# Group norm of a state-space mixer: the root and the reciprocal move from a 128x16 tile into whole PSUM banks, and the halves of the output projection are exchanged

## The chip, the core and the metric

The kernel runs on one core of a Trainium2 chip. The metric is the device time in microseconds (us), here the median of the runs shown. Five engines work side by side and wait for one another through semaphores: TensorE (PE, matrix products, with its weight loads shown as PEld), VectorE (DVE), ScalarE (ACT), GpSimd (POOL), and SyncE (SP), which here only issues transfers. Each engine takes its instructions in the order written.

## The reference, cut to what matters

The program is two transformer-like blocks on 512 tokens of width 1024; the change lies in the second one, in the norm over groups that closes the state-space branch and in the product that follows:

```python
y = y.reshape(b, L, D_INNER) * jax.nn.silu(z)                  # D_INNER = 2048
yg = y.reshape(b, L, N_GROUPS, D_INNER // N_GROUPS)            # 4 groups of 512
yg = yg * lax.rsqrt(jnp.mean(yg * yg, axis=-1, keepdims=True) + NORM_EPS)
y = yg.reshape(b, L, D_INNER) * ssm_norm_w
y_ssm = y @ w_ssm_out                                          # 2048 x 1024
merged = sigmoid(g_conv) * y_conv + sigmoid(g_ssm) * y_ssm
return merged @ w_out
```

## The kernel before, in words

**Layout.** Everything is held transposed: the 128 partitions are features, the 512 columns of a tile are the tokens. A chunk is 128 features. `y_ssm` has 16 chunks, four to each group, so a group's sum of squares goes over four chunks and over the partitions.

**Weights and products.** All weights come as one stream of panels of 128x2048 fp32 (1 MB), in the order written in `weight_stream`. SP loads panel p into slot p % 2 (L418) as soon as panel p - 2 is used up by POOL. ACT rounds it to `w_hi` (`round_weights`, L1259), and POOL then writes the rest, `w_lo = w_raw - w_hi`, in four pieces (L454) and signals after the last. Operands are split in the same way: ACT writes `b_hi` or `a_hi`, DVE writes `b_lo` or `a_lo`. A tile of 128x512 outputs over eight chunks is then 24 matmuls: 16 with `w_hi` (L504 and L505) and 8 with `w_lo` (L511), 5.44 us together. It needs `w_hi` at its first matmul and `w_lo` at its 17th. Two tiles use one panel. Where an operand is just becoming ready, `tile_pair` runs both tiles of a panel together, chunk by chunk: 16 matmuls with `hi` (L542), 16 with `w_lo` (L551), 16 with `lo` (L558). Results go round four PSUM banks `gemm_bank`, and a bank has to be emptied before it is used again. The other four banks, `aux`, serve all else.

**Order around the change.** It is written out by hand, engine by engine. PE: eight tiles of the convolution's projection (panels `P_CONV` + 0 to 3), four gate tiles (`P_GATE2` + 0, 1), then the state-space output projection: the pair and six tiles over `b_hi`/`b_lo` (`P_SSM` + 0 to 3, results `T_SSM` + 0 to 7) and as much over `a_hi`/`a_lo` (`P_SSM` + 4 to 7), then the last projection. Before, the first of these halves takes `y_ssm` chunks 8 to 15, the second chunks 0 to 7; DVE adds the two results (L2376), so their order changes nothing but rounding.

**The group norm before.** ACT squares the four chunks of group m (L1653), DVE adds them (L2343), and PE sums over the partitions with the squares as the stationary operand and one column of ones moving, four matmuls of 128x1 per group (`group_sum`, L1081). All four groups' sums land in 16 columns of `aux[0]`, tokens on the partitions. Once all are there, ACT takes the root of 128x16 (L1670) and DVE the reciprocal (L2349). PE then spreads each column over a bank again, as a product of the broadcast column with the identity: eight matmuls for groups 2 and 3 after the first two gate tiles (L1102), eight for groups 0 and 1 after the last gate tile (L1110). DVE multiplies `y_ssm` by weight and spread factor (`y_operand`, L2356), ACT rounds (L1682 into `b_hi`, L1685 into `a_hi`), DVE takes the low part (L2360).

**What stands in ACT's queue here.** After each of the first two panels of its gates, ACT does two sigmoids from the banks (L1677), `round_weights`, then four chunks of `b_hi` (L1682). After these come all eight `a_hi` (L1685), and only behind them the copies of `T_SSM` + 0 and 1 (L1690) and the rounding of panel `P_SSM` + 2. `after(p, t)` is `round_weights` for panel p + 2.

Of the kernel before, what the change touches and what calls it, by code (L numbers as in the profile page):

```python
# [9 lines left out]
ACT = mybir.ActivationFunctionType  # L10
# [3 lines left out]
P = 128  # L14
S = 512
D = 1024
KC = D // P
# [3 lines left out]
QT = S // P  # L21
# [4 lines left out]
GROUPS = 4  # L26
# [69 lines left out]
def build(nc, x_in, w_in, cols_in, poolw_in, ada_in, c_in, out):  # L96

    A_USE_SSM = 4 * KC
    A_USE_FFN = A_USE_SSM + KC
    B_USE_CONV = KC + MLP_GROUPS * KC  # L100
    B_USE_SSM = B_USE_CONV + KC
# [3 lines left out]
    with ExitStack() as ctx:  # L105
        def sb(name, shape, dt=F32):
            return ctx.enter_context(nc.sbuf_tensor(name, shape, dt))

        def sem(name):
            return ctx.enter_context(nc.semaphore(name))  # L110
# [83 lines left out]
        shift_out = new_part[:, 0:2]  # L194
        rinv2 = sb("rinv2", [P, QT])
        one_gain2 = sb("one_gain2", [P, 2])
        group_inv = sb("group_inv", [P, GROUPS * QT])
        group_root = sb("group_root", [P, GROUPS * QT])
        sq = sb("sq", [P, 2, S])
        dist_at = nc.sbuf_base  # L200
        row_b = sb("row_b", [P, 2, S])
# [24 lines left out]
        eps = sb("eps", [P, 2])  # L226
# [132 lines left out]
        ln_silu = sem("ln_silu")  # L359
        groot_ready = sem("groot_ready")  # L360
        ginv_ready = sem("ginv_ready")
        gspread_done = sem("gspread_done")
        yop_raw = sem("yop_raw")
        gc_ready = sem("gc_ready")
        gs_ready = sem("gs_ready")
# [131 lines left out]
        def _(pe):  # L497
# [578 lines left out]
            def group_sum(m):  # L1076
                pe.wait_ge(group_step, 3 * m + 3)
                if m == 0:
                    pe.wait_ge(root_ready, 6)
                for j in range(QT):  # L1080
                    mm = pe.matmul(aux[0][:, 4 * m + j:4 * m + j + 1], y_sq[0][:, j * P:(j + 1) * P], ones[:, 0:1],  # L1081
                                   start=(m == 0 and j == 0), stop=(m == 3 and j == QT - 1), skip_group_check=True)
                mm.then_inc(sq_read, 1)

            for m in range(4):
                full(P_CONV + m, T_CONV + 2 * m, b_hi, b_lo,
# [4 lines left out]
            for m in range(2):  # L1091
                if m == 0:
                    tile(0, P_GATE2, T_GATE2, 0, 0, wide(0), a_hi, a_lo, first=True)
                    group_sum(3)
                    tile(0, P_GATE2, T_GATE2 + 1, 0, 0, wide(1), a_hi, a_lo)
                else:
                    full(P_GATE2 + m, T_GATE2 + 2 * m, a_hi, a_lo)
                if m == 0:
                    pe.wait_ge(ginv_ready, 1)
                    for q in (2, 3):  # L1100
                        for j in range(QT):
                            mm = pe.matmul(aux[q][:, j * P:(j + 1) * P],  # L1102
                                           group_inv[:, 4 * q + j:4 * q + j + 1].to_broadcast([P, P]), ident[:, :],
                                           start=True, stop=True)
                        mm.then_inc(gspread_done, 1)
            pe.wait_ge(centered, 8)
            pe.wait_ge(ln_raw, 8)
            for q in (0, 1):
                for j in range(QT):
                    mm = pe.matmul(aux[q][:, j * P:(j + 1) * P],  # L1110
                                   group_inv[:, 4 * q + j:4 * q + j + 1].to_broadcast([P, P]), ident[:, :],
                                   start=True, stop=True)
                mm.then_inc(gspread_done, 1)

            for m in range(4):
                full(P_SSM + m, T_SSM + 2 * m, b_hi, b_lo,
# [136 lines left out]
        def _(act):  # L1253
# [9 lines left out]
            def load_table(func):  # L1263

                nonlocal tables
                act.activation(table_out[:, tables:tables + 1], eps[:, 0:1], func)
                tables += 1
# [391 lines left out]
            for j in range(4):  # L1659
                t = T_GATE + j  # L1660
                act.wait_ge(bank_free[t % 4], free_value(t))
                act.activation(g_ssm[:, j, :], g_ssm[:, j, :], ACT.Sigmoid).then_inc(gs_ready, 1)
            for m in range(4):
                if m:
                    after(P_CONV + m, T_CONV + 2 * m)
                if m < 3:
                    group_squares(m + 1)
            load_table(ACT.Sqrt)
            act.wait_ge(sq_read, GROUPS)
            act.activation(group_root[:, :], aux[0][:, 0:GROUPS * QT], ACT.Sqrt, bias=eps[:, 0:1],  # L1670
                           scale=1.0 / (4 * P)).then_inc(groot_ready, 1)

            for m in range(2):
                for j in range(2):
# [91 lines left out]
        def _(dve):  # L1766
# [566 lines left out]
                                  ALU.subtract).then_inc(b_lo_ready, 1)  # L2333
            gated_outputs(GROUPS - 1)

            for k in range(KC):
                t = T_CONV + k
                if k % 2 == 0:
                    for n in range(1, 4):
                        dve.wait_ge(sq_ready, 4 * KC + 2 * k + n)  # L2340
                        if n > 1:
                            dve.wait_ge(group_step, 3 * (k // 2) + n - 1)
                        dve.tensor_tensor(y_sq[0], y_sq[0], y_sq[n], ALU.add).then_inc(group_step, 1)  # L2343
                dve.wait_ge(gc_ready, k + 1)
                dve.wait_ge(tile_done, t + 1)
                dve.tensor_tensor(g_conv[:, k, :], g_conv[:, k, :], gemm_bank[t % 4][:, :], ALU.mult) \
                    .then_inc(bank_free[t % 4], 1)
            dve.wait_ge(groot_ready, 1)
            dve.reciprocal(group_inv[:, :], group_root[:, :]).then_inc(ginv_ready, 1)  # L2349

            def y_operand(first, value, hi, hi_sem, hi_base, lo, lo_sem, spreads):

                dve.wait_ge(gspread_done, spreads)
                for k in range(KC):
                    f = first + k
                    dve.scalar_tensor_tensor(value[:, k, :], y_ssm[:, f, :], col("ssm_norm_w", f),  # L2356
                                             aux[f // 4][:, :], ALU.mult, ALU.mult).then_inc(yop_raw, 1)
                for k in range(KC):
                    dve.wait_ge(hi_sem, hi_base + k + 1)
                    dve.tensor_tensor(lo[:, k, :], value[:, k, :], hi[:, k, :].bitcast(F32),  # L2360
                                      ALU.subtract).then_inc(lo_sem, 1)

            dve.wait_ge(ln_silu, KC)
            dve.wait_ge(tile_done, T_GATE2)
            y_operand(8, b_raw, b_hi, b_hi_ready, B_USE_SSM, b_lo, b_lo_ready, 2)
            dve.wait_ge(tile_done, T_SSM)
            dve.wait_ge(b_lo_ready, B_USE_SSM + 1 + KC)
            y_operand(0, a_raw, a_hi, a_hi_ready, A_USE_SSM, a_lo, a_lo_ready, 4)

            for k in range(KC + 1):  # L2370
                if k < KC:
# [145 lines left out]
def panels(w, kc, mc):  # L2517

    n = w.shape[1] // (mc * P)
    return w.reshape(kc, P, n, mc * P).transpose(2, 1, 0, 3).reshape(n, P, kc * mc * P)  # L2520
# [8 lines left out]
def weight_stream(v):  # L2529

    def pick(w, chunks):
        return np.concatenate([w[:, c * P:(c + 1) * P] for c in chunks], axis=1)

    w_in, up, down = v["w_in"], v["w_up"], v["w_down"]
    stream = [panels(pick(w_in, [4 + i, 8 + i, 12 + i, i] + [16 + 4 * i + j for j in range(4)]), KC, 2)
              for i in range(PAIRS)]
    stream += [panels(v["w_branch_attn"], 4, 4), panels(v["w_branch_pool"], 4, 4), panels(v["w_out"], KC, 2)]
    for g in range(MLP_GROUPS):
        stream += [panels(up[:, g * D:(g + 1) * D], KC, 2), panels(down[g * D:(g + 1) * D, :], KC, 2)]
    w = v["w_in_2"]  # L2540
    z0, x0 = 16, 32
    dt0 = (x0 + 24) * P
    dt = np.zeros((D, 2 * P), np.float32)
    dt[:, 0:SSM_HEADS] = w[:, dt0:dt0 + SSM_HEADS]
    stream.append(panels(dt, KC, 2))
    gates = w[:, dt0 + SSM_HEADS:]
    for g in range(GROUPS):
        stream.append(panels(pick(w, [2 * g, 8 + 2 * g, 2 * g + 1, 8 + 2 * g + 1]
                                  + [x0 + 4 * g + j for j in range(4)] + [x0 + 16 + g, x0 + 20 + g]), KC, 2))
        stream.append(panels(pick(gates, [2 * g, 2 * g + 1]), KC, 2))  # L2550
        stream.append(panels(pick(w, [z0 + 4 * g + j for j in range(4)]), KC, 2))
    stream += [panels(pick(gates, range(8, 12)), KC, 2), panels(v["w_conv_out_2"], KC, 2),
               panels(pick(gates, range(12, 16)), KC, 2),
               panels(v["w_ssm_out_2"][D:], KC, 2), panels(v["w_ssm_out_2"][:D], KC, 2), panels(v["w_out_2"], KC, 2)]
    ffn, ffn_down = v["w_ffn_in_2"], v["w_ffn_down_2"]
    for g in range(FFN_GROUPS):
        chunks = range(FC * g, FC * g + FC)
        stream.append(panels(pick(ffn, [c + half for c in chunks for half in (0, FFN_GROUPS * FC)]), KC, 2))
        rows = np.zeros((16 * P, D), np.float32)
        rows[:FC * P] = ffn_down[FC * P * g:FC * P * (g + 1)]  # L2560
        stream.append(panels(rows, 16, 1))
    return np.ascontiguousarray(np.concatenate(stream, axis=0))
# [51 lines left out]
```

## Time and profile before

| | |
|---|---|
| time, median of 3 runs | 1696.14 us (1695.92 to 1697.41) |
| profiled execution, span | 1694.9 us; its own time outside the span isn't given, the median lies 1.24 us above the span |
| PE busy | 1684.5 us, 99% of the span |
| DVE, ACT, POOL busy | 52%, 42%, 47% |
| granted TensorE clock, mean | 0.997 |
| stretch of the change | about 1130 to 1245 us from the span's start |

The span is the time from the first to the last instruction of one execution, recorded by the profiler. "Busy" counts work only, not waits. Durations of neighbouring matmuls overlap, since they are pipelined, so what a matmul costs is read from the distance between starts, not from its own duration. Bracketed text at the end of a timeline row is the idle time before the instruction, and what ended it.

### The profile page before, as it was taken

Reading aid. Unit: us, or ns where it says so; the run is one execution under the profiler, and the core shown is the slowest. Engines: PE = TensorE matmul, PEld = TensorE weight load, DVE = VectorE, ACT = ScalarE, POOL = GpSimd, SP = SyncE. Lnnn points to the kernel's source line nnn. Section 1 sums busy time; section 2 is a strip of 40 time slices with the busy share of each in tenths; the row PEclk is TensorE's granted clock in tenths of the full one; section 3 lists DMA queues with packets and bytes.
Section 4 is the critical chain, followed back from the end, with each engine's and each line's share of the span. In section 5 each row is a group of like instructions: output and inputs, shape, how many; then the busy total and the mean of one; then the engine's idle time right before and its main releaser. Section 6 shows DMA issues by size and latency. Waiting matters only on the chain.

```text
span 1694.9 us, 21874 instructions
## 1 busy us (share of the span) xinstructions
PE 1684.5 (99%) x7963; PEld 1374.6 (81%) x7963; DVE 874.7 (52%) x1365; ACT 706.1 (42%) x977; POOL 793.1 (47%) x605
## 2 busy tenths in 40 slices
PE   9999999999999999999999999999999999999998
PEld 7777778788888888888878888788888888888887
DVE  6234374563616167797897878863355511101113
ACT  5333364431313134456464554784424422222232
POOL 2434354444545455543434344444545544654453
PEclk9999999999999999999999999999999999999999
DMA  5222222274636342233222332222222222332232
GB/s 187 99 75 74 74 104 82 81 261 157 229 117 225 122 151 100 93 106 125 100 100 101 117 104 99 99 75 99 76 99 100 76 98 99 129 127 91 99 124 100
DMA packets 32540, 193.84 MB, mean 114 GB/s; under 512 B 3648, under 2 KB 5696, under 8 KB 13792
## 3 DMA queue, kind: packets, MB, share of 16 engines
q1 hardware_dynamic: 25376, 158.89, 26.5%
q10 hardware_dynamic: 7104, 34.15, 5.8%
q8 instruction: 38, 0.62, 0.1%
q14 instruction: 22, 0.18, 0.0%
HBM read 190.86 MB, written 2.16 MB: 114 GB/s over the span
## 4 chain that ended last, share of the span: by engine, by line
PE 98%; DMA 0%; DVE 0%; ACT 0%; SPq 0%; issue 0%; DVEq 0%
PE gemm_bank L511 25%; PE gemm_bank L504 25%; PE gemm_bank L505 25%; PE gemm_bank L542 4%; PE gemm_bank L558 4%; PE gemm_bank L551 3%; PE gemm_bank L546 1%; PE gemm_bank L789 1%; PE aux_bank L975 1%; PE aux_bank L655 1%; PE aux_bank L980 1%; PE aux_bank L960 1%; PE aux_bank L681 1%; PE aux_bank L672 1%; DMA w_raw<-weights_dram 0%; PE aux_bank L953 0%
## 5 line engine op out<-in xcount | busy, mean ns | idle before, releaser
L454 POOL TENSOR_TENSOR w_lo<-w_raw,w_hi 128x512 fp32r<-128x512 f32 x580 | 771.5, 1362 | 881.6 <-ACT w_hi L1259 870.4
L504 PE MATMUL gemm_bank<-a_hi,w_hi 128*128 128x512 f32 x1008 | 402.6, 399 | 0.0
L505 PE MATMUL gemm_bank<-a_lo,w_hi 128*128 128x512 f32 x1008 | 393.2, 390 | 0.0
L1259 ACT ACTIVATE w_hi<-w_raw 128x2048 fp32r<-128x2048 f32 x145 | 276.5, 1907 | 187.1 <-PE gemm_bank L511 122.7
L504 PE MATMUL gemm_bank<-b_hi,w_hi 128*128 128x512 f32 x688 | 267.8, 389 | 0.0
L505 PE MATMUL gemm_bank<-b_lo,w_hi 128*128 128x512 f32 x688 | 267.7, 389 | 0.0
L511 PE MATMUL gemm_bank<-a_hi,w_lo 128*128 128x512 f32 x1024 | 258.7, 395 | 0.0
L511 PEld LDWEIGHTS gemm_bank<-a_hi,w_lo 128*128 128x128 f32 x1024 | 190.2, 188 | 45.0 <-issue 6.2
L504 PEld LDWEIGHTS gemm_bank<-a_hi,w_hi 128*128 128x128 f32 x1008 | 189.3, 188 | 43.9 <-issue 5.6
L505 PEld LDWEIGHTS gemm_bank<-a_lo,w_hi 128*128 128x128 f32 x1008 | 189.4, 188 | 39.4 <-issue 1.9
L2161 DVE SCALAR_TENSOR_TENSOR aux_bank<-scratch,gcol,aux_bank 128x511 f32<-128x511 f32 (+15 forms) x240 | 165.8, 734 | 14.2 <-ACT aux_bank L1485 11.9
L511 PE MATMUL gemm_bank<-b_hi,w_lo 128*128 128x512 f32 x688 | 170.6, 389 | 0.0
L511 PEld LDWEIGHTS gemm_bank<-b_hi,w_lo 128*128 128x128 f32 x688 | 129.1, 188 | 26.8
L505 PEld LDWEIGHTS gemm_bank<-b_lo,w_hi 128*128 128x128 f32 x688 | 129.2, 188 | 26.8
L504 PEld LDWEIGHTS gemm_bank<-b_hi,w_hi 128*128 128x128 f32 x688 | 129.1, 188 | 26.7
L2461 DVE TENSOR_TENSOR arena<-arena,gemm_bank 128x512 f32<-128x512 f32 x21 | 14.4, 688 | 174.6 <-PE gemm_bank L511 173.1
L2394 DVE SCALAR_TENSOR_TENSOR h<-gemm_bank,mod,h 128x512 f32<-128x512 f32 x23 | 17.3, 751 | 108.6 <-PE gemm_bank L511 104.9
L504 PE MATMUL gemm_bank<-f_hi,w_hi 128*128 128x512 f32 x165 | 64.2, 389 | 0.0
L505 PE MATMUL gemm_bank<-f_lo,w_hi 128*128 128x512 f32 x165 | 64.2, 389 | 0.0
L1735 ACT ACTIVATE f_hi<-arena 128x512 f32 (+1 forms) x22 | 13.9, 632 | 115.9 <-DVE arena L2461 115.0
L2202 DVE SCALAR_TENSOR_TENSOR sq<-gemm_bank,gcol,sq 128x511 f32<-128x511 f32 (+2 forms) x72 | 53.8, 748 | 13.2 <-ACT sq L1505 11.5
L1393 ACT ACTIVATE b_hi<-gemm_bank 128x512 fp32r<-128x512 f32 x31 | 18.6, 599 | 100.5 <-DVE gemm_bank L2006 100.5
(414 smaller groups left out, 2133.4 us busy)
## 6 DMA issues: line engine op xcount, KB each, us to landing
w_raw<-weights_dram SPq DMA_DIRECT2D x146, 1024.0 KB, 4.7
arena<-ada_dram ACTq DMA_DIRECT2D x32, 768.0 KB, 4.7
acc<-cum_rows ACTq DMA_DIRECT2D x8, 512.0 KB, 3.7
h<-x_t_dram SPq DMA_DIRECT2D x8, 256.0 KB, 5.9
row_b<-cum_rows ACTq DMA_DIRECT2D x4, 512.0 KB, 4.8
scratch<-cum_rows ACTq DMA_DIRECT2D x4, 512.0 KB, 4.2
out_t_dram<-a_raw SPq DMA_DIRECT2D x7, 256.0 KB, 2.2
w_raw<-weights_dram SPq DMA_DIRECT2D x4, 256.0 KB, 5.2
```

The costliest lines, as they stand in the source:

```text
L454: ins = pool.tensor_tensor(wlo[s][:, w], raw[s][:, w], whi[s][:, w].bitcast(F32), ALU.subtract)
L504: pe.matmul(gemm_bank[bank][:, :], whi[slot][:, w], hi[:, k, :], start=(n == 0), stop=False)
L505: pe.matmul(gemm_bank[bank][:, :], whi[slot][:, w], lo[:, k, :], start=False, stop=False)
L511: mm = pe.matmul(gemm_bank[bank][:, :], wlo[slot][:, blk * P:blk * P + P], hi[:, k, :], start=False, stop=(n == last))
L542: pe.matmul(gemm_bank[t % 4][:, :], whi[panel % 2][:, w], hi[:, k, :], start=(n == 0), stop=False)
L551: pe.matmul(gemm_bank[t % 4][:, :], wlo[panel % 2][:, blk * P:blk * P + P], hi[:, k, :], start=False, stop=False)
L558: mm = pe.matmul(gemm_bank[t % 4][:, :], whi[panel % 2][:, blk * P:blk * P + P], lo[:, k, :], start=False, stop=(n == last))
L1259: act.activation(whi[panel % 2][:, :], raw[panel % 2][:, :], ACT.Copy).then_inc(w_hi_ready, 1)
L1393: act.activation(b_hi[:, j, :], bank, ACT.Square).then_inc(b_hi_ready, 1)
L2161: dve.scalar_tensor_tensor(aux[q][:, d:S], u_buf[:, q, 0:S - d], gc(G_CONV_W + CONV_TAPS * q + CONV_TAPS - 1 - d), aux[q][:, d:S], ALU.mul ...
L2202: ins = dve.scalar_tensor_tensor(acc[:, d:S], bank[:, 0:S - d], gc(G_SSM_W + SSM_TAPS * n + SSM_TAPS - 1 - d), acc[:, d:S], ALU.mult, ALU.add)
L2394: dve.scalar_tensor_tensor(hk, gemm_bank[t % 4][:, :], g_, hk, ALU.mult, ALU.add).then_inc(h_ready, 1)
```

## The change

- `group_sum(m)` becomes one product per group: 128x128 ones as the stationary operand, the 128x512 sum of squares moving, into the whole bank `aux[m]`. Each partition of the bank then holds the sum for each token, so nothing has to be spread. For m = 1 PE waits also for `ln_raw` (the bank's readers of before).
- ACT takes the root in the bank, in place, 128x512, once per group; `group_root(m)` stands behind `group_squares(m + 1)`, and the load of the table for the root stands ahead of the loop.
- DVE takes the reciprocal in the bank, in place, 128x512, once per group: groups 0 and 1 within the loop over the convolution's tiles (after k = 3 and k = 5), groups 2 and 3 between the two calls of `y_operand`.
- The sixteen matmuls that spread the factors are gone, with their semaphore.
- The first half of the output projection (operand b) takes chunks 0 to 7, the second (operand a) chunks 8 to 15, and the weight stream exchanges the two halves of `w_ssm_out_2`.

```diff
@@ PE
-                for j in range(QT):
-                    mm = pe.matmul(aux[0][:, 4 * m + j:4 * m + j + 1], y_sq[0][:, j * P:(j + 1) * P], ones[:, 0:1],
-                                   start=(m == 0 and j == 0), stop=(m == 3 and j == QT - 1), skip_group_check=True)
-                mm.then_inc(sq_read, 1)
+                if m == 1:
+                    pe.wait_ge(ln_raw, KC)
+                pe.matmul(aux[m][:, :], ones[:, :], y_sq[0], start=True, stop=True).then_inc(sq_read, 1)
...
-                if m == 0:
-                    pe.wait_ge(ginv_ready, 1)
-                    for q in (2, 3):
-                        for j in range(QT):
-                            mm = pe.matmul(aux[q][:, j * P:(j + 1) * P],
-                                           group_inv[:, 4 * q + j:4 * q + j + 1].to_broadcast([P, P]), ident[:, :],
-                                           start=True, stop=True)
-                        mm.then_inc(gspread_done, 1)
-            pe.wait_ge(centered, 8)
-            pe.wait_ge(ln_raw, 8)
-            for q in (0, 1):
...                                      (the same eight matmuls for groups 0 and 1)
@@ ACT
+            def group_root(m):
+                act.wait_ge(sq_read, m + 1)
+                act.activation(aux[m][:, :], aux[m][:, :], ACT.Sqrt, bias=eps[:, 0:1], scale=1.0 / (4 * P)) \
+                    .then_inc(groot_ready, 1)
+
+            load_table(ACT.Sqrt)
             for m in range(4):
                 if m:
                     after(P_CONV + m, T_CONV + 2 * m)
                 if m < 3:
                     group_squares(m + 1)
-            load_table(ACT.Sqrt)
-            act.wait_ge(sq_read, GROUPS)
-            act.activation(group_root[:, :], aux[0][:, 0:GROUPS * QT], ACT.Sqrt, bias=eps[:, 0:1],
-                           scale=1.0 / (4 * P)).then_inc(groot_ready, 1)
+                group_root(m)
@@ DVE
+            def group_inverse(m):
+                dve.wait_ge(groot_ready, m + 1)
+                dve.reciprocal(aux[m][:, :], aux[m][:, :]).then_inc(ginv_ready, 1)
...
-            dve.wait_ge(groot_ready, 1)
-            dve.reciprocal(group_inv[:, :], group_root[:, :]).then_inc(ginv_ready, 1)
+                if k in (3, 5):
+                    group_inverse(k // 2 - 1)
...
-            y_operand(8, b_raw, b_hi, b_hi_ready, B_USE_SSM, b_lo, b_lo_ready, 2)
+            y_operand(0, b_raw, b_hi, b_hi_ready, B_USE_SSM, b_lo, b_lo_ready, 2)
+            group_inverse(2), group_inverse(3)
             dve.wait_ge(tile_done, T_SSM)
             dve.wait_ge(b_lo_ready, B_USE_SSM + 1 + KC)
-            y_operand(0, a_raw, a_hi, a_hi_ready, A_USE_SSM, a_lo, a_lo_ready, 4)
+            y_operand(8, a_raw, a_hi, a_hi_ready, A_USE_SSM, a_lo, a_lo_ready, 4)
@@ weight_stream
-               panels(v["w_ssm_out_2"][D:], KC, 2), panels(v["w_ssm_out_2"][:D], KC, 2), panels(v["w_out_2"], KC, 2)]
+               panels(v["w_ssm_out_2"][:D], KC, 2), panels(v["w_ssm_out_2"][D:], KC, 2), panels(v["w_out_2"], KC, 2)]
```

## Rows read from the trace of the kernel before

**Rows 1.** The page: busy time of each engine, and the granted clock by slices.
```profile
PE 1684.5 (99%) x7963; PEld 1374.6 (81%) x7963; DVE 874.7 (52%) x1365; ACT 706.1 (42%) x977; POOL 793.1 (47%) x605
...
PEclk9999999999999999999999999999999999999999
```

**Rows 2.** Waits of PE over the whole span: total, times, longest, in us.
```profile
PE gemm_bank L789 <- ACT a_hi L1371: 1.4, 1, 1.4
...
PE aux_bank L1214 <- ACT sq L1759: 0.9, 1, 0.9
```

**Rows 3.** Timeline of PE, group sums and first spread: start, us, engine, line, operation.
```profile
1142.69 1.98 PE L511 MATMUL gemm_bank<-b_hi,w_lo 128*128 128x512 f32 x8
1148.13 1.98 PE L511 MATMUL gemm_bank<-b_hi,w_lo 128*128 128x512 f32 x8
1149.95 0.95 PE L1081 MATMUL aux_bank<-ones,sq 128*128 128x1 f32 x8
1154.49 1.98 PE L511 MATMUL gemm_bank<-b_hi,w_lo 128*128 128x512 f32 x8
...
1172.65 1.98 PE L511 MATMUL gemm_bank<-a_hi,w_lo 128*128 128x512 f32 x8
1174.47 1.95 PE L1102 MATMUL aux_bank<-ident,group_inv 128*128 128x128 f32 x16
1179.91 1.98 PE L511 MATMUL gemm_bank<-a_hi,w_lo 128*128 128x512 f32 x8
```

**Rows 4.** Timeline of PE around the product of ones in the earlier layer norm.
```profile
1095.25 1.02 PE L1055 MATMUL aux_bank<-poolw,ones 128*128 128x512 f32 x2
1095.71 2.41 PE L511 MATMUL gemm_bank<-a_hi,w_lo 128*128 128x512 f32 x8
1097.96 0.40 PE L504 MATMUL gemm_bank<-a_hi,w_hi 128*128 128x512 f32 x1
```

**Rows 5.** Timeline of PE, second spread and start of the output projection.
```profile
1187.17 1.95 PE L1110 MATMUL aux_bank<-ident,group_inv 128*128 128x128 f32 x16
1188.87 3.91 PE L542 MATMUL gemm_bank<-b_hi,w_hi 128*128 128x512 f32 x16
1192.61 3.79 PE L551 MATMUL gemm_bank<-b_hi,w_lo 128*128 128x512 f32 x16
...
1214.37 1.98 PE L511 MATMUL gemm_bank<-b_hi,w_lo 128*128 128x512 f32 x8
...
1232.51 3.79 PE L542 MATMUL gemm_bank<-a_hi,w_hi 128*128 128x512 f32 x16
```

**Rows 6.** Timeline of ACT, last gate tile to the rounding of the third panel.
```profile
1187.37 0.60 ACT L1677 ACTIVATE arena<-gemm_bank 128x512 f32<-128x512 f32 x1 [4.84 <-PE gemm_bank L511]
1187.86 1.90 ACT L1259 ACTIVATE w_hi<-w_raw 128x2048 fp32r<-128x2048 f32 x1
1189.66 2.18 ACT L1682 ACTIVATE b_hi<-scratch 128x512 fp32r<-128x512 f32 x4
1197.66 5.24 ACT L1685 ACTIVATE a_hi<-a_raw 128x512 fp32r<-128x512 f32 x8 [5.81 <-DVE a_raw L2356]
1202.81 1.07 ACT L1690 ACTIVATE arena<-gemm_bank 128x512 f32<-128x512 f32 x2
1203.76 1.92 ACT L1259 ACTIVATE w_hi<-w_raw 128x2048 fp32r<-128x2048 f32 x1
```

**Rows 7.** Timeline of DVE, low parts of b, then operand a.
```profile
1190.32 6.47 DVE L2360 TENSOR_TENSOR b_lo<-scratch,b_hi 128x512 fp32r<-128x512 f32 x4 [5.75 <-ACT b_hi L1682]
1196.88 5.36 DVE L2356 SCALAR_TENSOR_TENSOR a_raw<-arena,cols,aux_bank 128x512 f32<-128x512 f32 x8
1202.15 4.90 DVE L2360 TENSOR_TENSOR a_lo<-a_raw,a_hi 128x512 fp32r<-128x512 f32 x8
```

**Rows 8.** Timeline of POOL: low parts of the second and third panel of the projection, and a later one.
```profile
1189.84 6.40 POOL L454 TENSOR_TENSOR w_lo<-w_raw,w_hi 128x512 fp32r<-128x512 f32 x4 [7.63 <-ACT w_hi L1259]
1205.76 6.18 POOL L454 TENSOR_TENSOR w_lo<-w_raw,w_hi 128x512 fp32r<-128x512 f32 x4 [9.52 <-ACT w_hi L1259]
1213.43 5.03 POOL L454 TENSOR_TENSOR w_lo<-w_raw,w_hi 128x512 fp32r<-128x512 f32 x4 [1.49 <-ACT w_hi L1259]
```

**Rows 9.** Reciprocals on DVE, by line: duration in ns, lowest, median, highest.
```profile
L2120 DVE RECIPROCAL aux_bank<-scratch x1: 961/961/961, 699.0 to 699.0; 128x128 f32<-128x128 f32 x1
...
L2349 DVE RECIPROCAL group_inv<-group_root x1: 253/253/253, 1169.4 to 1169.4; 128x16 f32<-128x16 f32 x1
```

**Rows 10.** Timeline of ACT in the convolution's tiles.
```profile
1142.01 1.91 ACT L1259 ACTIVATE w_hi<-w_raw 128x2048 fp32r<-128x2048 f32 x1
...
1166.76 1.28 ACT L1266 ACT_TABLE_LOAD   x1
```

More of the change, by code:

```diff
@@ L196, in build @@
         one_gain2 = sb("one_gain2", [P, 2])
-        group_inv = sb("group_inv", [P, GROUPS * QT])
-        group_root = sb("group_root", [P, GROUPS * QT])
         sq = sb("sq", [P, 2, S])
@@ L361, in build @@
         ginv_ready = sem("ginv_ready")
-        gspread_done = sem("gspread_done")
         yop_raw = sem("yop_raw")
@@ L1097, in _ @@
                     full(P_GATE2 + m, T_GATE2 + 2 * m, a_hi, a_lo)
-                if m == 0:
-                    pe.wait_ge(ginv_ready, 1)
-                    for q in (2, 3):
-                        for j in range(QT):
-                            mm = pe.matmul(aux[q][:, j * P:(j + 1) * P],
-                                           group_inv[:, 4 * q + j:4 * q + j + 1].to_broadcast([P, P]), ident[:, :],
-                                           start=True, stop=True)
-                        mm.then_inc(gspread_done, 1)
-            pe.wait_ge(centered, 8)
-            pe.wait_ge(ln_raw, 8)
-            for q in (0, 1):
[L1109 to L1113, printed above, removed]
             for m in range(4):
@@ L2347, in _, with y_operand @@
                     .then_inc(bank_free[t % 4], 1)
-            dve.wait_ge(groot_ready, 1)
-            dve.reciprocal(group_inv[:, :], group_root[:, :]).then_inc(ginv_ready, 1)
-            def y_operand(first, value, hi, hi_sem, hi_base, lo, lo_sem, spreads):
-                dve.wait_ge(gspread_done, spreads)
+                if k in (3, 5):
+                    group_inverse(k // 2 - 1)
+            def y_operand(first, value, hi, hi_sem, hi_base, lo, lo_sem, inverses):
+                dve.wait_ge(ginv_ready, inverses)
                 for k in range(KC):
```

## The prediction

> **What bounds the kernel now.** First the page: PE is busy for 1684.5 of 1694.9 us, at a granted clock in the top tenth in every slice [rows 1]. Then PE's waits: the longest is 1.4 us, and none lies in the stretch of the change [rows 2]. So here each matmul taken away is worth its whole distance between starts, as long as everything PE is fed with still comes in time. What the other engines save is worth nothing, but what they are given may make them late. So I read, third, the timeline of each engine between 1187 and 1215 us for margins.
>
> **PE's own work.** The timeline of PE gives the price of each part as a distance between starts less the 5.44 us of a tile (1148.13 - 1142.69).
> - A group sum: 1154.49 - 1148.13 = 6.36, so 0.92 us each [rows 3].
> - The product of ones that replaces it stands in the trace already, in the layer norm: 1097.96 - 1095.25 = 2.71 us from its start to the next tile, of which eight matmuls at 5.44/24 = 0.227 take 1.81; it costs 0.90 us [rows 4]. Four of them against four sums save 0.08 us. I take it as it stands; it could be 0.1 us off either way in each of the four.
> - First spread: 1179.91 - 1172.65 - 5.44 = 1.82 us [rows 3].
> - Second spread: 1.70 us to the next start, and that next run of 16 takes 3.74 where 3.63 is its pace, so 1.81 us [rows 5].
>
> Together PE loses 3.7 us of work. That would be all if nothing became late.
>
> **What becomes late first: `b_hi`.** The last gate tile ends at 1187.17. ACT then does its sigmoid and the rounding of panel `P_SSM` + 1, and starts chunks 4 to 7 of `b_hi` at 1189.66, the last ending at 1191.84 [rows 6]. PE took the second spread meanwhile. The first of these chunks was wanted eight matmuls after 1188.87, at 1190.68, and was there at about 1190.3, when DVE begins its low part [rows 7]. Counted from the end of the last gate tile, ACT's chain does not change: its chunks 0 to 3 still come between the panels, and making `b_raw` starts earlier, as no spread precedes it. But PE now wants chunk 4 of operand b 1.8 us sooner. In the clock of the new kernel the gate tile ends at 1187.17 - 1.82 - 0.08 = 1185.27; the last chunk is there at 1189.94, its two matmuls end at 1190.45 with the signal, and L551 starts there, where it started at 1192.61 before. So 2.15 us of the 3.7 are left at this point: about 1.5 us is a new wait.
>
> **What becomes late next: `w_lo` of panel `P_SSM` + 2.** This is the term that decides. Behind the four low parts of b, DVE now has two reciprocals of 128x512 before it can make operand a. Behind operand a stand, on ACT, eight `a_hi`, two copies of result banks and only then the rounding of that panel, and behind it POOL's low part. I follow it in the trace: low parts of b end at 1196.79, operand a starts at 1196.88, ACT follows to about 1202.9, copies to 1203.8, rounding to 1205.7, POOL 1205.76 to 1211.94 [rows 6 to 8]. From the end of the last gate tile that chain takes 1211.94 - 1187.17 = 24.77 us. PE wanted the result at 1214.37 [rows 5], a margin of 2.43 us.
>
> The price of a reciprocal: 253 ns for 16 columns and 961 ns for 128 [rows 9], so 6.32 ns for a column more. For 512 columns 961 + 384 x 6.32 = 3.39 us, 6.78 us for two. The bounds: at the least what a plain operation of this shape takes, 5.36/8 = 0.67 us each [rows 7], if the length went unused; at the most the 128-column row four times over, 3.84 us. I take 3.39 us, since both lengths lie on it and only the distance is extended. Both rows read SBUF, and the new ones read PSUM; I take no surcharge, as L2356 reads the bank at 0.67 us apiece.
>
> The chain then takes 24.77 + 6.78 = 31.55 us and ends at 1185.27 + 31.55 = 1216.82. So the L511 of tile `T_SSM` + 4 starts at 1216.8 and not at 1214.37: **2.45 us later than before**. Seen as waits: the tile started at 1214.37 - 3.63 = 1210.74 before, so after the 2.15 us PE wants `w_hi` at 1208.6; it gets it at 1185.27 + (1205.7 - 1187.17) + 6.78 = 1210.6 (a wait of 2 us), then wants `w_lo` at 1214.2 and gets it at 1216.8 (about 2.6 us). With the 1.5 us at `b_hi`, 6.1 us of waits against 3.7 us of work removed. POOL's 6.18 us holds some contention with DVE's low parts of a, which keep their place relative to the chain; without any it takes 5.03 us [rows 8], so the end may come up to 1.15 us sooner.
>
> **Behind it.** `P_SSM` + 3 gets its `w_lo` by 1216.8 + 5 to 1216.8 + 6.4, and is wanted about 11 us after 1216.8: enough. SP may load panel `P_SSM` + 4 from 1216.8 on, 4.9 us later than before, but ACT rounds it only when tile `T_SSM` + 5 is done, about 7 us later. Operand a, whole at about 1212, is wanted at 1232.5 and later [rows 5]. So nothing else waits, and nothing gives the loss back.
>
> **Edits I cost at nothing.** The table load ahead of the loop (1.28 us and its small use) and the root of group 0 (about 0.6 us, by the bank row of L1677 [rows 6]) delay the rounding that started at 1142.01 [rows 10] by 2.1 us; POOL needs 5.03 us behind it, so its low part is whole at about 1151.1, wanted at 1154.49 [rows 3, 8]. Cover of 3.4 us; if it were gone, each us beyond would count in full. The later roots delay roundings by 0.6 us with more cover. Reciprocals 0 and 1 run while DVE waits for tiles. The wait for `ln_raw` was met long before. The sigmoid table is loaded as often as before, and the exchanged weights have the same sizes.
>
> **A rule that speaks against it.** The two rows of reciprocals lie 708 ns apart for 112 columns [rows 9]. The Trainium skill ("VectorE: DVE Perf Modes", "First, the fixed hardware budget" and "Specifications") describes the reciprocal as an iterative divide with a repeat count of 8 on an engine of 0.96 GHz. As eight cycles for a column that would be, as an estimate from that page, 8.3 ns a column or 4.27 us for 512. By that the two would take 8.5 us, the sum would be 1.8 us longer, and the kernel would end at 1700.4. The trace's 6.32 ns disagrees.
>
> **Result.** 2.45 us onto the profiled span of 1694.9 is 1697.35 us. The median of the runs shown lies 1.24 us above that span, so the time is **1698.6 us**, +0.14%. About 0.2% (3.4 us) is what a measurement of this kernel can tell from no change, so this is "the same", on the slow side.
>
> **Rivals.**
> 1. All the work removed is gained: 1696.14 - 3.7 = 1692.4 us, faster. For it: PE is 99% busy with no wait here. Against it: `b_hi` 4 had 0.4 us of margin and loses 1.8. Both late chains must turn out shorter: chance 0.05.
> 2. The reciprocal is cheap or only the first wait is real: 2.15 us gained, 1694.0 us. It decides below (2.43 + 1.9 - 2.15) / 2 = 1.1 us a reciprocal. Against it, the 128-column row alone took 0.96 us. With what lies between it and my forecast (POOL without contention, 1697.4), chance 0.12.
> 3. Slower: the reciprocal in place in PSUM needs more than a SBUF row's slope. Place: the same chain, between DVE's low parts of b and operand a. Each tenth of a us counts twice. At 3.84 us (four times the 128-column row) it gives 0.9 us more, 1699.5; at 4.3 us, as if the slope were a third higher, 1.8 us more, 1700.4. It decides from 3.9 us each. Against it, L2120 writes PSUM already at the lower slope. Chance 0.17, and 0.03 for mishaps such as the earlier cover of 3.4 us failing.
> 4. The granted clock could fall in the new waits. Nothing speaks for it: the slices stay in the top tenth, also at the 1.4 us wait. Within rival 3's chance.
>
> The forecast itself has the remaining 0.63; its own range is 1697.2 to 1699.4. The range over cases runs from 1695.4 to 1700.6, leaving out rival 1, most of rival 2 and the mishaps. Faster by over 0.2% is below 1692.75: 0.05. Slower is above 1699.5: 0.20. Same: 0.75.
>
> **What would show it.** Four products of ones at about 0.9 us in PE's timeline, no matmuls behind the gate tiles; a wait of some 1.5 us in L542 for `b_hi`; two waits at `T_SSM` + 4, for ACT's `w_hi` and POOL's `w_lo`, of 2 and 2.6 us; reciprocals of 3.4 us, two of them directly ahead of operand a on DVE. I am wrong if the reciprocals differ from 3.4 us by more than 0.4, or if PE shows no wait at `T_SSM` + 4.

## The result, and the profile after

The changed kernel takes 1701.03 us (median of 16 runs, 1698.53 to 1701.98) against 1696.14 us (16 runs, 1695.54 to 1697.41): a ratio of 1.0026, 95% interval 1.0019 to 1.0032. The forecast was 1698.6 us, 2.5 us more than before, and 4.9 us were measured: the direction of its sum was right and its size too small by half. The profiled execution took 1700.93 us, with a span of 1699.2.

PE's waits over the whole span, in the columns of [rows 2], now hold three in the stretch of the change, where there were none:

```profile
PE gemm_bank L508 <- POOL w_lo L451: 2.3, 1, 2.3
PE gemm_bank L501 <- ACT w_hi L1239: 1.5, 1, 1.5
...
PE gemm_bank L539 <- ACT b_hi L1665: 1.2, 1, 1.2
...
PE aux_bank L1194 <- DVE dist L2389: 0.3, 1, 0.3
```

PE's timeline shows where each lies (line numbers are 3 lower than before in this part: L508 was L511, L539 was L542). It answers to [rows 3 and 5]:

```profile
1148.16 1.98 PE L508 MATMUL gemm_bank<-b_hi,w_lo 128*128 128x512 f32 x8
1149.97 1.02 PE L1079 MATMUL aux_bank<-sq,ones 128*128 128x512 f32 x2
...
1154.50 1.98 PE L508 MATMUL gemm_bank<-b_hi,w_lo 128*128 128x512 f32 x8
...
1183.50 1.98 PE L508 MATMUL gemm_bank<-a_hi,w_lo 128*128 128x512 f32 x8
1185.31 1.97 PE L539 MATMUL gemm_bank<-b_hi,w_hi 128*128 128x512 f32 x8
1188.47 2.29 PE L539 MATMUL gemm_bank<-b_hi,w_hi 128*128 128x512 f32 x8 [1.19 <-ACT b_hi L1665]
1190.60 3.81 PE L548 MATMUL gemm_bank<-b_hi,w_lo 128*128 128x512 f32 x16
...
1206.94 1.98 PE L508 MATMUL gemm_bank<-b_hi,w_lo 128*128 128x512 f32 x8
1210.38 0.50 PE L501 MATMUL gemm_bank<-b_hi,w_hi 128*128 128x512 f32 x1 [1.46 <-ACT w_hi L1239]
...
1216.60 3.50 PE L508 MATMUL gemm_bank<-b_hi,w_lo 128*128 128x512 f32 x8 [2.28 <-POOL w_lo L451]
...
1223.78 1.98 PE L508 MATMUL gemm_bank<-b_hi,w_lo 128*128 128x512 f32 x8
...
1236.47 3.79 PE L539 MATMUL gemm_bank<-a_hi,w_hi 128*128 128x512 f32 x16
```

The row at 1216.60 is the one to look at. Eight matmuls that take 1.98 us in the other rows take 3.50 there, with no wait among them. The table by windows says why; its columns are the length of the window, busy time and count of PE, the granted clock, and the share and GB/s of DMA:

```profile
1214.00:1216.00 2.00, 0.32 (x2) 1.00 0.00 0
1216.00:1217.00 1.00, 0.40 (x2) 0.97 0.00 0
1217.00:1218.00 1.00, 1.00 (x4) 0.50 0.32 57
...
1219.00:1220.00 1.00, 1.00 (x4) 0.50 1.04 442
1220.00:1221.00 1.00, 1.00 (x5) 0.82 0.80 336
1221.00:1222.00 1.00, 1.00 (x6) 1.00 0.00 0
```

Right behind the third wait the granted clock is 0.50, the 1.2 GHz level, and then 1.00 again. With the parts of the two windows at the ends (0.97 and 0.82) that is about 3.4 us.

The chain on the other engines, with its two reciprocals, answers to [rows 7 and 9] on DVE, to [rows 6] on ACT and to [rows 8] on POOL:

```profile
1188.45 6.46 DVE L2347 TENSOR_TENSOR b_lo<-scratch,b_hi 128x512 fp32r<-128x512 f32 x4 [4.41 <-ACT b_hi L1665]
1194.83 6.56 DVE L2321 RECIPROCAL aux_bank<-aux_bank 128x512 f32<-128x512 f32 x2
1201.53 5.36 DVE L2343 SCALAR_TENSOR_TENSOR a_raw<-arena,cols,aux_bank 128x512 f32<-128x512 f32 x8
...
1208.41 1.91 ACT L1239 ACTIVATE w_hi<-w_raw 128x2048 fp32r<-128x2048 f32 x1
...
1210.40 11.10 POOL L451 TENSOR_TENSOR w_lo<-w_raw,w_hi 128x512 fp32r<-128x512 f32 x8 [16.04 <-ACT w_hi L1239]
```

The last row holds the low parts of two panels; the first four of its eight pieces are those that PE waits for until 1216.60.

**Where the time went.** I measure from the low products of the last gate tile to the first matmul over operand a: 1185.35 to 1232.51, 47.16 us before, and 1183.50 to 1236.47, 52.97 us after. Against PE's unhindered pace (45.34 us, measured below), the after trace has four losses, each a distance between starts less the distance at full pace:

| place | distance | at full pace | lost |
|---|---|---|---|
| `b_hi` (1185.31 to 1190.60) | 5.29 | 3.62 | 1.67 |
| `w_hi` (1206.94 to 1210.38) | 3.44 | 1.81 | 1.63 |
| `w_lo` (1210.38 to 1216.60) | 6.22 | 3.63 | 2.59 |
| clock (1216.60 to 1223.78) | 7.18 | 5.44 | 1.74 |
| sum, and 52.97 - 45.34 | | | 7.63 |

The last term is not all clock. Behind a wait of 0.9 to 2.3 us at the full clock, the same distance is 5.57 us in e4 and 5.60 in e7, 0.13 and 0.16 over pace; so about 1.6 us of the 1.74 are the price of the clock's fall.

### The profile page after: what moved, and what is told of

It reads as the page before. It is cut to its first block, busy times and chain, and to the rows that moved or that the text cites. A ratio compares the mean times of both kernels' runs of the same rounds, so it can differ in the third digit from the quotient of the medians.

```text
span 1699.2 us, 21768 instructions
## 1 busy us (share of the span) xinstructions
PE 1683.7 (99%) x7907; PEld 1369.8 (81%) x7907; DVE 891.2 (52%) x1368; ACT 707.4 (42%) x980; POOL 794.0 (47%) x605
## 4 chain that ended last, share of the span: by engine, by line
PE 96%; issue 1%; DVE 1%; POOL 1%; DMA 0%; ACT 0%; SPq 0%; DVEq 0%; POOLq 0%
PE gemm_bank L508 25%; PE gemm_bank L501 25%; PE gemm_bank L502 24%; PE gemm_bank L539 4%; PE gemm_bank L555 4%; PE gemm_bank L548 2%; PE gemm_bank L543 1%; PE gemm_bank L786 1%; PE aux_bank L972 1%; PE aux_bank L652 1%; PE aux_bank L977 1%; PE aux_bank L957 1%; POOL w_lo L451 1%; PE aux_bank L678 1%; PE aux_bank L669 1%
## 5 line engine op out<-in xcount | busy, mean ns | idle before, releaser
L508 PE MATMUL gemm_bank<-a_hi,w_lo 128*128 128x512 f32 x1024 | 258.7, 395 | 0.0
L508 PEld LDWEIGHTS gemm_bank<-a_hi,w_lo 128*128 128x128 f32 x1024 | 190.2, 188 | 44.9 <-issue 6.2
L508 PE MATMUL gemm_bank<-b_hi,w_lo 128*128 128x512 f32 x688 | 172.1, 392 | 2.3 <-POOL w_lo L451 2.3
L508 PEld LDWEIGHTS gemm_bank<-b_hi,w_lo 128*128 128x128 f32 x688 | 130.0, 189 | 29.7 <-POOL w_lo L451 2.7
```

Of the source, the lines that this page charges most:

```text
L508: mm = pe.matmul(gemm_bank[bank][:, :], wlo[slot][:, blk * P:blk * P + P], hi[:, k, :], start=False, stop=(n == last))
```

## The experiments

The theory: two reciprocals of 3.3 us stand in the chain from the last gate tile over DVE, ACT and POOL to `w_lo` of panel `P_SSM` + 2; the removal of the second spread uncovers `b_hi`; and the idle time makes the clock fall. The rivals: the loss is in PE's or ACT's side of the change, or the clock is what costs, however long the waits.

### Both late chains, one at a time

**e1_recips_early**: the reciprocals of groups 2 and 3 ahead of the low parts of b.

```diff
 (in y_operand, behind its eight products)
+                for m in between:
+                    group_inverse(m)
...
-            y_operand(0, b_raw, b_hi, b_hi_ready, B_USE_SSM, b_lo, b_lo_ready, 2)
-            group_inverse(2), group_inverse(3)
+            y_operand(0, b_raw, b_hi, b_hi_ready, B_USE_SSM, b_lo, b_lo_ready, 2, between=(2, 3))
```

> The changed kernel with the reciprocals of groups 2 and 3 taken ahead of the low parts of operand b (behind its eight products), where DVE stood idle for 4.8 us. Theory (two reciprocals of 3.3 us in the chain DVE, ACT, POOL behind operand a make w_lo of the third projection panel late): that chain ends 6.6 us sooner, near 1210, ahead of the 1212.4 at which PE wants it. Both waits at T_SSM + 4 and the low clock behind them go; the 1.2 us wait for b_hi stays. Time 1694.1 us, about 2.0 below before and 6.9 below the changed kernel. Rival (the loss comes from PE's or ACT's side of the change, the products of ones or the roots in the banks): unchanged, 1701 us.

Measured: 1694.64 us (11 runs), ratio 0.9991 (0.9982 to 1.0) to before. The timeline of DVE shows the reciprocals in the place where it had stood idle, and operand a begins right behind the low parts of b:

```profile
1166.97 5.35 DVE L2343 SCALAR_TENSOR_TENSOR scratch<-arena,cols,aux_bank 128x512 f32<-128x512 f32 x8
1172.24 6.57 DVE L2321 RECIPROCAL aux_bank<-aux_bank 128x512 f32<-128x512 f32 x2
...
1188.04 6.46 DVE L2349 TENSOR_TENSOR b_lo<-scratch,b_hi 128x512 fp32r<-128x512 f32 x4 [4.25 <-ACT b_hi L1665]
1194.58 5.35 DVE L2343 SCALAR_TENSOR_TENSOR a_raw<-arena,cols,aux_bank 128x512 f32<-128x512 f32 x8
```

PE's waits between 1130 and 1345 are down to the one expected:

```profile
PE gemm_bank L539 <- ACT b_hi L1665: 1.2, 1, 1.2
```

So the products of ones and the roots in the banks are not what costs. Moving 6.6 us of DVE work took 6.4 us from the kernel, but not one for one: the table above has 4.2 us for the two waits behind it and 1.74 for what follows them.

**e4_one_recip**: the same with `between=(2,)`, and the reciprocal of group 3 left ahead of operand a.

> The changed kernel with only the reciprocal of group 2 moved ahead of the low parts of b; that of group 3 stays ahead of operand a. Theory: the chain to w_lo shrinks by 3.3 us, from 1216.6 to 1213.3, where PE wants it at 1212.4: a wait of 0.9 us there, none for w_hi, no fall of the clock. 1.07 us are gained at that place against before: 1695.1 us. Rival (the low clock behind the waits is what costs, whatever their length): 1696.5 us or more with a low clock in the stretch.

Measured: 1695.99 us (11 runs), ratio 0.9999 (0.999 to 1.0008). The wait for `w_lo` is 0.87 us, as expected. The next tile starts 5.57 us later, and the granted clock is 1.00 in every window from 1208 to 1224:

```profile
1212.61 2.11 PE L508 MATMUL gemm_bank<-b_hi,w_lo 128*128 128x512 f32 x8 [0.87 <-POOL w_lo L451]
1218.18 1.98 PE L508 MATMUL gemm_bank<-b_hi,w_lo 128*128 128x512 f32 x8
```

The dose is graded: none, one, two reciprocals in the chain give 1694.64, 1695.99 and 1701.03 us. The time itself came 0.9 us above the expected 1695.1.

**e2_bhi_early**: all eight chunks of `b_hi` after the first gate panel.

```diff
-                for k in range(4 * m, 4 * m + 4):
+                for k in range(KC if m == 0 else 0):
                     act.wait_ge(yop_raw, k + 1)
```

> The changed kernel with all eight chunks of b_hi rounded by ACT after its first gate panel; the reciprocals stay where they are. Theory: the wait for b_hi (1.2 us) goes; and since DVE's low parts of b no longer wait for the second gate panel, they end near 1187 and not 1194.9, so the reciprocals, operand a, a_hi, the rounding and POOL all come some 7.5 us sooner, and w_lo is there at about 1208.5 where PE wants it at 1210.7. All 3.7 us of removed PE work are gained: 1692.4 us, no waits of PE in the stretch. Rival (only the wait for b_hi is cured, the reciprocals still cost their 6.6 us in the chain from the last gate tile): the waits at T_SSM + 4 grow by as much as the b_hi wait shrinks, 1701 us.

Measured: 1692.93 us (11 runs), ratio 0.9981 (0.9972 to 0.999), 0.5 us above the expected time, and no wait of PE between 1130 and 1345. Its timeline gives the unhindered pace, 1228.12 - 1182.78 = 45.34 us:

```profile
1182.78 1.98 PE L508 MATMUL gemm_bank<-a_hi,w_lo 128*128 128x512 f32 x8
1184.60 3.79 PE L539 MATMUL gemm_bank<-b_hi,w_hi 128*128 128x512 f32 x16
1188.22 3.79 PE L548 MATMUL gemm_bank<-b_hi,w_lo 128*128 128x512 f32 x16
...
1228.12 3.79 PE L539 MATMUL gemm_bank<-a_hi,w_hi 128*128 128x512 f32 x16
```

One edit cures both chains. DVE's low parts of b no longer wait for ACT's second gate panel, so the reciprocals, still in their place, start 2.9 us behind PE's last L508 of the gates (1185.67 - 1182.78) and not 11.3 (1194.83 - 1183.50), 8.4 us sooner:

```profile
1176.87 8.88 DVE L2347 TENSOR_TENSOR b_lo<-scratch,b_hi 128x512 fp32r<-128x512 f32 x8 [4.84 <-ACT b_hi L1665]
1185.67 6.56 DVE L2321 RECIPROCAL aux_bank<-aux_bank 128x512 f32<-128x512 f32 x2
```

**e3_both**: both edits together.

> Both edits, reciprocals ahead of the low parts of b and all of b_hi after the first gate panel. Theory: 1692.4 us, as with the second edit alone, with more margin for w_lo; the ceiling is PE's own work less 3.7 us. Rival (the two waits are not independent, one edit undoes the other's room, for instance DVE's eight low parts of b are now too late for PE at 1192.5): 1693 to 1695 us.

Measured: 1693.7 us (11 runs, 1692.57 to 1694.12), ratio 0.9983 (0.9974 to 0.9992). The time is 1.3 us above the expected one and within the 1693 to 1695 us of the rival. The trace speaks against the rival's cause all the same: the same stretch takes 45.34 us again, PE waits for nothing in it, and of the 0.8 us between the profiled executions of e3 and e2 (1693.36 and 1692.59) all is there long before the change (640.53 against 639.76 us for the same L508 of an earlier tile). The intervals of both ratios overlap. So no gain of the second edit shows where the first stands.

### One part alone, in the kernel before

**e7_before_recips**: the kernel before with two such reciprocals added, spreads and all else kept.

```diff
             y_operand(8, b_raw, b_hi, b_hi_ready, B_USE_SSM, b_lo, b_lo_ready, 2)
+            for m in (2, 3):
+                dve.reciprocal(aux[m][:, :], aux[m][:, :])
```

> The kernel before, with its sixteen spreads, and two reciprocals of 128x512 in PSUM added between operand b and operand a on DVE (results unused). Theory: this part of the change alone delays w_lo of P_SSM + 2 from 1211.9 to 1218.6, wanted at 1216.0 after a wait of 1.6 us for w_hi, so 4.2 us more at that place, and 1.7 more where the clock falls: 1700.3 to 1702.1 us, at or above the changed kernel. Rival (the loss needs the removal of the spreads too): 1697 us or less.

Measured: 1700.76 us (10 runs), ratio 1.0024 (1.0015 to 1.0034). The waits are the two of the chain, without that for `b_hi`:

```profile
PE gemm_bank L511 <- POOL w_lo L454: 2.3, 1, 2.3
...
PE gemm_bank L504 <- ACT w_hi L1259: 1.0, 1, 1.0
```

So two reciprocals at this place bring both waits of the chain without anything else of the change, and cost 4.4 us. That this is near the 4.9 us of the change is in part chance, as the two are made up differently: e7 keeps the 3.7 us of PE work and has no wait for `b_hi`. In its profiled execution (1699.77 us) the clock stayed at 1.00 from 1130 to 1340, where the expectation had a fall, and the place came out 3.8 us late (1217.39 - 1186.38 against 1214.37 - 1187.17 [rows 5]).

**e9_spread_early**: the kernel before with all sixteen spread matmuls after the first two gate tiles; PE's work is unchanged.

```diff
+                    pe.wait_ge(centered, 8)
+                    pe.wait_ge(ln_raw, 8)
-                    for q in (2, 3):
+                    for q in (2, 3, 0, 1):
...
-            pe.wait_ge(centered, 8)
-            pe.wait_ge(ln_raw, 8)
-            for q in (0, 1):
...                                       (its eight matmuls)
```

> The kernel before, with all sixteen spread matmuls after the first two gate tiles and none after the last gate tile; PE's work is the same. Theory (the second spread covered the rounding of b_hi 4 to 7, so its removal alone brings the 1.2 us wait at L542): PE waits 1.2 us there, and the chain to w_lo, which starts at the end of the last gate tile and so comes 1.8 us later, is still in time (margin 2.4 - 1.8 + 1.2 = 1.8 us). Time 1697.5 us. Rival (the 1.2 us wait of the changed kernel has another cause, such as the earlier sigmoids or the roots): no change, 1696.3 us.

Measured: 1698.14 us (11 runs), ratio 1.001 (1.0001 to 1.0019), 1.8 us over the kernel before beside it (1696.33) and 0.6 above the expected time, with the very wait:

```profile
1189.46 1.98 PE L542 MATMUL gemm_bank<-b_hi,w_hi 128*128 128x512 f32 x8
1192.63 2.29 PE L542 MATMUL gemm_bank<-b_hi,w_hi 128*128 128x512 f32 x8 [1.19 <-ACT b_hi L1676]
1194.76 3.81 PE L551 MATMUL gemm_bank<-b_hi,w_lo 128*128 128x512 f32 x16
```

1194.76 - 1189.46 is 5.30 us, 1.67 us over pace, as in the changed kernel. The expectation had counted only the 1.2 us that the profile calls a wait. The second spread had stood where PE would have waited anyway, so by itself its removal gains 1.81 - 1.67 = 0.14 us.

### The clock

**e5_fill_low**: the changed kernel, with 18 transposes of the identity (results unused) in the wait for `w_lo`. **e6_fill_high**: 12 of them in the wait for `w_hi`, none in the other.

```diff
+            def keep_busy(count):
+                for _ in range(count):
+                    pe.transpose(aux[0][:, 0:P], ident[:, :], ident[:, :])
...
+                    keep_busy(0)        # e6: 12
+                    tile_high(0, P_SSM + 2, T_SSM + 4, 0, 0, wide(0), b_hi, b_lo, first=True)
+                    keep_busy(18)       # e6: 0
+                    tile_low(0, P_SSM + 2, T_SSM + 4, 0, wide(0), b_hi, first=True)
```

> The changed kernel with 18 transposes of the identity into a free bank (about 2.0 us of PE work, results unused) between the products with w_hi and those with w_lo of tile T_SSM + 4, where PE waited 2.3 us. They fit in the wait. Theory (the granted clock fell because PE stood idle here, which made the next eight matmuls 3.3 us long in place of 1.8 and the following one longer too): w_lo is used at 1216.6 as before, but at the full clock; the granted clock stays at 1.00 in 1216 to 1221, and the time falls by 1.7 us, to 1699.3, in all executions and not in some. Rival (the clock falls for all the idle time of the stretch together, or for another reason): the clock still falls there, 1701 us or a little more.

> The same with 12 transposes (about 1.4 us) ahead of tile T_SSM + 4, in the wait for w_hi, and none in the wait for w_lo. Theory that only the idle time directly ahead of the fall counts: the clock still falls at about 1217, 1701 us. Rival (it is the idle time of both waits together): the clock stays up, 1699.3 us.

Measured: e5 1699.05 us (11 runs, 1698.63 to 1700.0), ratio 1.0015 (1.0006 to 1.0024); e6 1700.51 us (11 runs, 1698.5 to 1701.09), ratio 1.002 (1.0011 to 1.0029). In e5 the products come as late as in the changed kernel, but near pace, and the granted clock is 1.00 in every window from 1216 to 1224:

```profile
1214.41 2.13 PE L1097 MATMUL aux_bank<-ident 128*128 128x128 f32 x18
1216.89 2.11 PE L508 MATMUL gemm_bank<-b_hi,w_lo 128*128 128x512 f32 x8 [0.35 <-POOL w_lo L451]
1222.46 1.98 PE L508 MATMUL gemm_bank<-b_hi,w_lo 128*128 128x512 f32 x8
```

In e6 the wait for `w_lo` is open, and the clock falls though PE was busy in the wait for `w_hi`. PE's timeline and the table by windows:

```profile
1208.31 1.47 PE L1097 MATMUL aux_bank<-ident 128*128 128x128 f32 x12
...
1216.15 3.14 PE L508 MATMUL gemm_bank<-b_hi,w_lo 128*128 128x512 f32 x8 [2.27 <-POOL w_lo L451]
1223.35 1.98 PE L508 MATMUL gemm_bank<-b_hi,w_lo 128*128 128x512 f32 x8
```

```profile
1217.00:1218.00 1.00, 1.00 (x4) 0.50 0.89 131
```

So useless PE work in one wait of 2.3 us gives back 2.0 us of the median, and 1.5 us against e6, which has the same split of the tile and was measured beside it.

The wait alone does not decide whether the clock falls. e7, whose profiled execution has a 2.3 us wait and no fall, shows it by rows, though its other waits are shorter (1.0 us for `w_hi`, none for `b_hi`). The times of single executions point the same way: of the changed kernel's 16, three took 1698.53 to 1699.09 us and thirteen 1700.3 to 1701.98; of e6's eleven, three 1698.5 to 1698.86 and eight 1700.32 to 1701.09; of e5's eleven, none was above 1700.0. That the clock fell in the upper groups and stayed in the lower ones would fit, but only the profiled executions have rows. The Trainium skill ("TensorE: Matmul & The Clock Gate", "What's actually happening") says that the activity is judged by a schedule which does not start with the kernel. Two groups of times of one kernel would fit that too; no run here shows it by rows.

### A faster version

**e8_sum_round**: e2 with the products of ones in the rounded format of the weights. The last add of each group writes the sum rounded, and the ones are copied once into that format.

```diff
-                        dve.tensor_tensor(y_sq[0], y_sq[0], y_sq[n], ALU.add).then_inc(group_step, 1)
+                        dve.tensor_tensor(sq_round[:, :] if n == 3 else y_sq[0], y_sq[0], y_sq[n], ALU.add).then_inc(group_step, 1)
...
-                pe.matmul(aux[m][:, :], ones[:, :], y_sq[0], start=True, stop=True).then_inc(sq_read, 1)
+                pe.matmul(aux[m][:, :], ones_round[:, :], sq_round[:, :], start=True, stop=True).then_inc(sq_read, 1)
```

> The changed kernel with all of b_hi rounded early (1692.93 us), and the four products of ones taken in the rounded format of the weights: the last of each group's three adds writes the sum of squares rounded, and the ones are copied once into that format. The 0.9 us of a product of 128x512 in full fp32 should become the 0.23 us of any 128x512 product with w_hi: 4 x 0.67 = 2.7 us less, 1690.2 us, if the chain to w_lo (ready near 1207.4 in that trace, wanted at 1210.0) still keeps pace; its first link follows the gate tiles, which come sooner too, so its margin of 2.5 us holds. Rival (the format change between neighbouring products costs PE something, or the chain becomes late): 1691 to 1693 us.

Measured: 1690.41 us (6 runs, 1690.1 to 1691.26), ratio 0.9967 (0.9955 to 0.9979). A product now costs 1152.58 - 1146.88 - 5.44 = 0.26 us for 0.90:

```profile
1146.88 1.98 PE L511 MATMUL gemm_bank<-b_hi,w_lo 128*128 128x512 f32 x8
1148.69 0.39 PE L1083 MATMUL aux_bank<-sq_round,ones_round 128*128 128x512 f32 x1
1152.58 1.98 PE L511 MATMUL gemm_bank<-b_hi,w_lo 128*128 128x512 f32 x8
```

It is the fastest of all, 5.9 us below the kernel before (1696.33 us beside it). It gives up precision in the sums of squares, which the version e2 keeps.

## Why the prediction was right, and where it fell short

**PE's work: right.** The product of ones costs 1154.50 - 1148.16 - 5.44 = 0.90 us, as read from the layer norm [rows 4]. The second half of the gate tiles begins without spreads, and the output projection starts at 1185.31, worked out as 1185.27.

**`b_hi`: right.** L548 starts at 1190.60, worked out as 1190.45. e9 shows that the removal of the second spread from its place is enough to bring the wait, e2 that the wait can be avoided.

**The chain to `w_lo`: right in mechanism and size.** It was to end at 1216.8; PE got `w_lo` at 1216.60. The reciprocals take 3.36 us each, for 3.39 worked out from the rows of 16 and 128 columns; a surcharge for working in place in PSUM doesn't show. Without them in the chain the loss is gone (e1), with one it is mostly gone (e4), and with nothing but them both of its waits are there (e7). The two waits were to be 2.0 and 2.6 us; as distances they are 1.63 and 2.59.

**The estimate under "A rule that speaks against it": refuted.** Its 4.27 us stand against 3.36 measured, 6.24 ns a column between 128 and 512 columns. In rival 3, a slope a third higher gives 4.2 us and not 4.3; nothing hangs on it.

**What failed: rival 4.** The prediction held the clock at its upper level, because it stayed there at the 1.4 us wait [rows 2] and in every slice [rows 1], and gave its fall no price and no chance of its own. In the profiled execution it fell, at a price of about 1.6 us of the 1.74, and the times of single executions would fit a fall in 13 of 16. That is the term missing from the sum. The three executions at 1698.53 to 1699.09 us lie near the forecast of 1698.6, as they should if the clock stayed up: the place is 2.23 us late (1216.60 against 1214.37), 0.1 to 0.2 us go in the first tile behind the wait, and 0.3 us in the last stretch. The median of 1701.03 lies 0.4 us beyond the top of the range of 1700.6, and by the bound of 1699.5 it is in the case "slower", which had 0.20, not in "the same", which had 0.75. The two lie close: the ratio's interval holds the 0.2% that was to part them.

"Nothing speaks for it" was a misreading, too. A slice of the page is 42 us long, and a fall of 3 us can't be seen in it: all 40 slices of the changed kernel's page read 9 as well. The kernel before has a fall of its own, which a table by windows shows (columns as above), with the granted clock at 0.50 from about 671.2 to 678.0:

```profile
666.00:671.00 5.00, 5.00 (x35) 1.00 0.47 161
671.50:677.50 6.00, 6.00 (x26) 0.50 0.14 29
678.50:684.00 5.50, 5.50 (x26) 1.00 0.38 156
```

PE has no wait between 640 and 690 there. It had gone from products of 512 columns to products of one or two columns at 668.65, and eight of these take 1.03 us before the fall and 1.85 in it:

```profile
669.47 1.03 PE L842 MATMUL aux_bank<-ones,acc 128*128 128x1 f32 x8
671.26 1.85 PE L842 MATMUL aux_bank<-ones,row_b 128*128 128x1 f32 x8
```

So the fall behind the new waits was open, and should have been priced with both levels, 8 x 0.227 = 1.8 us for each 3.6 us spent at the lower one. The earlier fall also moves times without any edit: it lasts some 6.7 us in the traces of both kernels and some 3.4 us in that of e2, which comes from 639.76 to 1130.22 in 490.46 us where the kernel before takes 491.26 (from 639.63 to 1130.89).

**Sum.** Of 1701.03 - 1696.14 = 4.9 us, 3.96 stand by 1236.47 in the profiled executions: 7.63 lost less 1.81 and 1.86 for both spreads and the cheaper sums. A further 0.3 us comes in the last stretch, as a wait of PE for an add of DVE; every trace with the change has it and none of the three of the kernel before (with e7 and e9), and its cause was not tracked down. That is the 4.3 us between the spans. The remaining 0.6 us is not the change: other executions of the kernel before with spans of 1694.8 to 1695.0 us took 1696.5 to 1696.8 us, so the profiled one was about 0.5 us above the median, and that of the changed kernel was 0.1 below its own. For the same reason the 1.24 us that the prediction put outside the span are too few; in the changed kernel's 16 executions it is 1.68 to 1.76 us.

## What to carry to other kernels

When one engine is busy for 99% of the time, taking work from it gains only what is not needed as cover: for each operation removed, ask who was finishing behind it. An operation moved to an idle engine has its price where it stands in that engine's queue; the same two reciprocals cost 6.4 us ahead of operand a, the clock's fall included, and nothing 20 us earlier. And a new wait of 2 us on TensorE has to be priced twice, once as a wait and once, with a chance, as matmuls at half the clock behind it. Whether the clock falls in a kernel is read from windows of a few us, not from the slices of the page.

## What was not expected of the hardware

- The granted clock fell to 0.50 for about 3.4 us behind a wait of only 2.3 us, with another of 1.5 us ending some 4 us earlier or with that one filled (e6). It stayed at 1.00 behind a wait of the same 2.3 us in e7.
- It fell without any wait of PE, at 671 us of the kernel before, behind 2.6 us of products of one or two columns.
- The same product of 128x512 costs PE 0.90 us in full fp32 (the changed kernel) and 0.26 us in the rounded format (e8); both are distances between starts.
